# A two-block transformer kernel: six plain projection blocks in place of four around the first attention, 34 Strassen blocks in place of 36

## The chip, the cores and the metric

One program runs on one core of a Trainium2 chip. The metric is device time in microseconds (us) for one launch; lower is better. The engines that matter are TensorE (PE, with its weight loads shown as PEld), VectorE (DVE), ScalarE (ACT), GpSimd (POOL, here mostly an issuer of DMAs) and SyncE (SP, an issuer of DMAs).

## The reference, cut to what matters

```
# d_model 1024, 1024 tokens, w_in has 40 column blocks of 256:
# blocks 0-3 sb_q, 4-7 sb_k, 8-11 sb_v, 12-15 sb_g, 16-31 r_q, r_k, r_v, r_g,
# blocks 32-35 m_sb, 36-39 m_ret
h = rms_norm(x, norm_gain)
proj = h @ w_in                                    # all ten outputs
out_a = merge_heads(stick_breaking_attention(rms_norm(q), rms_norm(k), v)) * silu(sb_g)   # 8 heads of 128
out_b = merge_heads(rms_norm(chunkwise_retention(rotary(q), rotary(k), v))) * silu(r_g)
merged = sigmoid(m_sb + b0) * (out_a @ w_branch_sb) + sigmoid(m_ret + b1) * (out_b @ w_branch_ret)
x = x + merged @ w_out
# then a second layer (gated linear attention + sliding window attention) and a feed-forward of 4096
```

## The kernel before, in words

Each product of h with one column block of w_in (256 columns, "a block") is done in one of two ways. Every operand is split into a high and a low part, and each product is made of three: high by high, high by low, low by high.

- **Strassen blocks** (n = 0 to NPROJ - 1, PE line 2785): seven half-size products of 4 x 3 = 12 matmuls with 512 columns, 84 matmuls in all, in PSUM banks 0 to 3 in turn (`product_bank`, bank (7n + o) % 4). DVE adds the products up, ACT applies what the block's kind asks for (norm, turn, silu, sigmoid, or nothing: "plain" in `proj_kind`), and POOL stores the block to the DRAM tensor `projections`. `content(n)` says where block n goes there, `proj_column` which columns of w_in it takes.
- **Plain blocks** (`gemm`, PE line 621, and `filler`, PE line 2891): four outputs of 24 matmuls, 96 matmuls in all. A matmul of a filler is called a pass.

After the last Strassen block comes the attention of the 8 heads, two heads ("a pair") at a time, 16 steps per pair (`sb_pair`, S = 0 to 15; the even steps are one head, the odd ones the other, with 1 to 8 blocks of 128 keys). In step S, PE makes the scores of step S + 2 (line 2863, and the mask, line 2865), turns the weights of step S (`turn`, 2872) and, after two steps of a head, multiplies by the values (`weigh`, 2844). ACT takes two sigmoids of the scores (`shares`, 1426 and 1429) and copies the turned weights out of banks 0 and 1 (`keep_first`, 1435); DVE makes a running product (`remaining`, 2061) and a product with it (`weights`, 2068). `turn(S)` waits for `weights(S)` and for `keep_first(S - 1)`. The scores of two steps fit in PSUM; bank 2 holds the attended output, bank 3 a background output.

Between these PE runs the passes of plain blocks, in an order written out by hand: `FILL_PASSES[i][S]` passes in step S of pair i, up to three of them ahead of `turn` ("early") and the rest behind `weigh`. When 24 passes are done, ACT copies bank 3 to a staging tile (`keep_filler`, 1442), POOL stores it (line 1117), and only then may the next output begin (`g_raw`). Before, two plain blocks of m_sb are made so, each over two pairs (48 passes for each of the pairs 0 to 2), and the last pair adds one output of the first covering block (72 passes).

After the last pair come the covering blocks (COVER and COVER + 1, two blocks of m_ret): they give PE work while ACT and DVE split the attended output into its parts (`s_hi` 1488, `s_lo` 2094). Then the branch product B1 (line 621 again) needs those parts and its own weights. SP loads weights in the order of use (`load_block`, 593): each load waits until the block two before it is done. The m_sb and m_ret gates are read back later by POOL (`gate_again`). The hidden layer of the feed-forward uses the same Strassen code with block numbers that go on from NPROJ.

Of the kernel before, what the change touches and what calls it, by code (L numbers as in the profile page):

```python
# [5 lines left out]
SEQ, DM = 1024, 1024  # L6
# [53 lines left out]
def build(nc, x, norm_gain, w_in, b_merge, sb_q_gain, sb_k_gain, ret_out_gain, w_branch_sb, w_branch_ret, w_out,  # L60
# [189 lines left out]
    with ctx:  # L250
# [18 lines left out]
        NPROJ = 36  # L269
        NORM0 = 3  # L270
        NHID = 15
        SB_GATE, SB_MERGE = 30, 34
# [4 lines left out]
        ms_d = nc.dram_tensor("merge_gate_sb", (P, KT // 2, SEQ), f32, kind="Internal").ap()  # L277
# [385 lines left out]
        pa_stored = [sem(f"pa_stored{u}") for u in range(2)]  # L663
        mg_in, mg_sig = [sem(f"merge_gate{j}_in") for j in range(4)], sem("merge_gate_sigmoid")
# [10 lines left out]
        L1, COVER, B1, B2, L5 = 0, 2, 4, 8, 12  # L675
        L6, L7, L8 = 16, 26, 30
# [53 lines left out]
        def proj_kind(n):  # L730
            return "plain" if n < NORM0 else "norm" if n < NORM0 + 8 else "turn" if n < NORM0 + 12 or 20 <= n < 24 else "plain" if n < 26 else "silu" if n < 34 else "sigmoid"

        def content(n):
            return 12 + n if n < NORM0 else n - NORM0 if n < NORM0 + 12 else n if n < 24 else n + 10 if n < 26 else n - 2 if n < 30 else n if n < 34 else n - 6

        def proj_column(n):
            m = content(n)
            return BC * (m if m < 12 else m + 4 if m < 28 else m + 8 if m < SB_GATE else m - SB_GATE + 12 if m < SB_MERGE else m - SB_MERGE + 32)
# [54 lines left out]
        HID0, HSUM0 = 32 + 4 * (F0 - 25), 32  # L793
# [9 lines left out]
        def form_stored(b, name):  # L803

            n, two = F0 + b, 16 * (b // 2 + 1)
            if name == "a11":
                return (pa_stored[0], 16 * 8 + two) if b % 2 else (c_stored[0], 16 * 28 + two)
            if name == "a22":
                return c_stored[1], 16 * 28 + 16 * (b + 1)
            if name in ("a12", "s3"):  # L810
                return c_stored[(2 if name == "a12" else 4) + n % 2], 16 * 14 + two
            q = ("s1", "s2", "s4").index(name)
            return q_stored[q], 16 * ((32 - q + 2) // 3) + 16 * (b + 1)
# [39 lines left out]
        def _(sp):  # L853
# [38 lines left out]
            load_block(sp, L1, 0, w1_d[:, :, 8, 2 * BC:3 * BC])  # L892
            sp.wait_ge(product_done, 7 * (NPROJ - 1) + 5)
            attention_values(0)
            load_block(sp, L1 + 1, 1, w1_d[:, :, 8, 3 * BC:4 * BC])
# [171 lines left out]
        def _(pool):  # L1067
# [16 lines left out]
            for n in range(NPROJ):  # L1084
                for j in range(4):
# [14 lines left out]
                    else:  # L1100
                        pool.wait_ge(first_ok, 32 + 4 * (n - 26) + j + 1)
# [6 lines left out]
            for i in range(4):  # L1108
# [16 lines left out]
            for j in range(4):  # L1125
                gate_again(proj_d[SB_MERGE].rearrange("p (c t) -> p c t", c=2), 0, j)
            for b in range(2):
                for j in COVER_ORDER[b]:
# [3 lines left out]
            for b in range(3):  # L1132
                for j in range(4):
                    pool.wait_ge(kept[j], kept_by(B1 + b))
                    if b:
                        gate_again(ms_d, 2 * b - 2, j)
                    else:
                        gate_again(proj_d[SB_MERGE + 1].rearrange("p (c t) -> p c t", c=2), 0, j)
            for u in range(2):
                pool.wait_ge(pa_stored[u], 16 * 8)  # L1140
# [98 lines left out]
        def _(act):  # L1239
# [107 lines left out]
            def gate_bias(n, ct):  # L1347
                c = COLS["merge"] + 8 + 2 * (n - 34) + ct
                return cols[:, c:c + 1] if n >= 34 else 0.0
# [18 lines left out]
            for n in range(1, NPROJ + 1):  # L1368
# [4 lines left out]
                if n == 26:  # L1373
                    act.preload_act_table_set("silu_and_others")
                elif n == 34:
# [42 lines left out]
            def sb_pair(i, n):  # L1418
# [34 lines left out]
                for S in range(16):  # L1453
# [36 lines left out]
            for s in range(2):  # L1490
                for v, j in enumerate(COVER_ORDER[s]):
                    act.wait_ge(gp_done, done(COVER + s, v))
                    act.wait_ge(pa_stored[j % 2], 16 * (4 + 2 * s + v // 2))
# [387 lines left out]
        def _(dve):  # L1881
            for j in range(4):
                dve.sem_inc(kept[j], 1)
            dve.sem_inc(gated, 4)
            dve.wait_ge(own_gain, 16)
# [157 lines left out]
            def end_of_pair(i):  # L2043

                dve.wait_ge(o_kept, 8 * i + 8)
                for j in range(4) if i % 2 else ():
# [1447 lines left out]
```

## Time and profile before

| | |
|---|---|
| median of 3 runs | 2438.62 us (2437.91 to 2439.53) |
| the profiled execution | 2438.28 us, its span 2436.5 us |
| PE busy | 2404.9 us, 12042 matmuls |
| PEld busy | 1973.6 us |
| DVE busy | 1613.6 us |
| ACT busy | 1030.9 us |
| Strassen blocks | about 47 to 743 us of the span |
| attention, 4 pairs | 743 to 962 us |
| covering outputs | 962 to 1000 us |

A busy share of PE is not PE at its peak: a matmul of 512 columns is shown with 0.39 us, though in a steady run one starts every 0.227 us. Rates of PE are therefore read from the time in which a run of matmuls goes by, divided by their number, and stalls from the idle time before a weight load.

### The profile page before, as it was taken

The numbers are of one execution on the slowest core, as the hardware profiler recorded it, in microseconds if no ns is written. First come the engines' busy times: TensorE is split into PE (matmuls) and PEld (weight loads), VectorE is DVE, ScalarE is ACT, GpSimd is POOL, SyncE is SP. The second block draws the span as 40 slices with busy tenths as digits, with TensorE's granted clock in tenths as the row PEclk, the third lists the DMA queues.
The fourth block names the chain that finished last, engine by engine and source line by source line (L and its number), as shares of the span: only waits on it lengthen the run. The fifth ranks groups of instructions, "written<-read, shape, count | busy, mean of one in ns | idle before, by whom it ended". The sixth has DMA issues, their size and how long they took to land.

```text
span 2436.5 us, 30593 instructions
## 1 busy us (share of the span) xinstructions
PE 2404.9 (99%) x12042; PEld 1973.6 (81%) x12042; DVE 1613.6 (66%) x2079; ACT 1030.9 (42%) x1751; POOL 238.9 (10%) x395
## 2 busy tenths in 40 slices
PE   7999999999999999999999999999999999999998
PEld 6888888888887777889888877887888888888887
DVE  7777656556556766377742654267567776789889
ACT  6466422233335656123422346234545444533334
POOL 2011111111110000100010003000001211100000
PEclk9999999999999999999999999999999999999999
DMA  4322333333334231734232410100333444673433
GB/s 154 100 104 100 108 104 108 100 108 108 108 123 145 79 116 63 262 100 178 78 115 89 130 35 20 41 30 18 115 123 123 162 147 158 242 259 141 156 122 120
DMA packets 141775, 285.90 MB, mean 117 GB/s; under 512 B 18470, under 2 KB 91744, under 8 KB 134848
## 3 DMA queue, kind: packets, MB, share of 16 engines
q1 hardware_dynamic: 109168, 175.45, 21.7%
q0 software_dynamic: 32464, 108.49, 12.6%
q8 instruction: 96, 1.57, 0.3%
q14 instruction: 47, 0.39, 0.1%
HBM read 200.02 MB, written 83.89 MB: 117 GB/s over the span
## 4 chain that ended last, share of the span: by engine, by line
PE 90%; DVE 5%; DMA 2%; ACT 1%; DVEq 1%; issue 1%; ACTq 0%; SPq 0%; POOL 0%
PE ps L2785 38%; PE ps L621 13%; PE ps L3466 8%; PE ps L3049 7%; PE ps L2844 2%; PE ps L2863 2%; PE ps L615 2%; PE ps L3356 2%; PE ps L2891 2%; PE ps L2872 1%; PE ps L3341 1%; PE ps L2752 1%; PE ps L2964 1%; PE ps L2979 1%; PE ps L3034 1%
## 5 line engine op out<-in xcount | busy, mean ns | idle before, releaser
L1991 DVE TENSOR_TENSOR proj_out<-ps,proj_out 128x512 f32<-128x512 f32 x334 | 223.3, 685 | 248.9 <-PE ps L2785 234.9
L2785 PE MATMUL ps<-a_hi,pw_hi 128*128 128x512 f32 x600 | 235.2, 392 | 0.0
L2785 PE MATMUL ps<-a_lo,pw_hi 128*128 128x512 f32 x600 | 233.5, 389 | 0.0
L2785 PE MATMUL ps<-t_hi,pw_hi 128*128 128x512 f32 x560 | 219.3, 392 | 0.0
L2785 PE MATMUL ps<-t_lo,pw_hi 128*128 128x512 f32 x560 | 218.0, 389 | 0.0
L2785 PE MATMUL ps<-a_hi,pw_lo 128*128 128x512 f32 x400 | 155.9, 390 | 0.0
L2785 PEld LDWEIGHTS ps<-a_lo,pw_hi 128*128 128x128 f32 x600 | 112.7, 188 | 23.0
L2785 PEld LDWEIGHTS ps<-a_hi,pw_hi 128*128 128x128 f32 x600 | 112.6, 188 | 22.9
L1264 ACT ACTIVATE pw_hi<-pw_raw 128x512 fp32r<-128x512 f32 x150 | 83.6, 621 | 107.4 <-DMA pw_raw<-in_w_in 61.8
L1918 DVE TENSOR_TENSOR pw_lo<-pw_raw,pw_hi 128x512 fp32r<-128x512 f32 x200 | 128.4, 683 | 0.2
L2785 PEld LDWEIGHTS ps<-t_lo,pw_hi 128*128 128x128 f32 x560 | 105.2, 188 | 21.5
L2785 PEld LDWEIGHTS ps<-t_hi,pw_hi 128*128 128x128 f32 x560 | 105.1, 188 | 21.3
L2061 DVE TENSOR_TENSOR_SCAN kept<-kept 128x128 f32<-128x128 f32 (+7 forms) x64 | 86.7, 1355 | 49.6 <-ACT kept L1426 49.6
L3466 PE MATMUL ps<-ws_hi,hidden_hi 128*128 128x512 f32 x288 | 112.3, 390 | 0.2 <-DVE gated_first L2658 0.2
L3466 PE MATMUL ps<-ws_hi,hidden_lo 128*128 128x512 f32 x288 | 112.1, 389 | 0.0
L3466 PE MATMUL ps<-ws_lo,hidden_hi 128*128 128x512 f32 x288 | 112.0, 389 | 0.0
L2785 PE MATMUL ps<-t_hi,ps_lo 128*128 128x512 f32 x280 | 109.1, 389 | 0.0
L2785 PE MATMUL ps<-t_hi,pw_lo 128*128 128x512 f32 x280 | 109.0, 389 | 0.0
L1102 POOL DMA_DIRECT2D projections<-proj_out x112 | 60.6, 541 | 480.9 <-ACT proj_out L1336 167.8
L1271 ACT ACTIVATE pw_hi<-ps_raw 128x512 fp32r<-128x512 f32 x150 | 87.9, 618 | 38.9 <-DVE ps_raw L1910 38.9
L3049 PE MATMUL ps<-w_hi,a_hi 128*128 128x512 f32 x256 | 101.5, 397 | 0.0
L601 DVE TENSOR_TENSOR w_lo<-w_raw,w_hi 128x2048 fp32r<-128x2048 f32 x26 | 59.5, 2288 | 61.5 <-ACT w_hi L597 54.9
(531 smaller groups left out, 6190.4 us busy)
## 6 DMA issues: line engine op xcount, KB each, us to landing
pw_raw<-in_w_in SPq DMA_DIRECT2D x36, 1024.0 KB, 5.8
projections<-proj_out POOLq DMA_DIRECT2D x112, 256.0 KB, 3.5
hidden_raw<-hidden_forms SPq DMA_DIRECT2D x28, 1024.0 KB, 4.8
pw_raw<-in_w_ff SPq DMA_DIRECT2D x16, 1024.0 KB, 6.0
w_quarter<-in_w_ff SPq DMA_DIRECT2D x16, 1024.0 KB, 6.8
hidden_forms<-proj_out POOLq DMA_DIRECT2D x56, 256.0 KB, 3.1
hidden_forms<-nb POOLq DMA_DIRECT2D x56, 256.0 KB, 3.4
w_raw<-in_w_in SPq DMA_DIRECT2D x10, 1024.0 KB, 5.2
```

The costliest lines, as they stand in the source:

```text
L601: dve.tensor_tensor(W_lo[s][:, :, :], W_raw[s][:, :, :], W_hi[s][:, :, :].bitcast(f32), ALU.subtract).then_inc(w_lo, 1)
L615: last = pe.matmul(bank[banks[j]][:, r * BC:(r + 1) * BC], a[:, k, t:t + P], w[s][:, k, :], start=(k == 0 and g == 0), stop=(k == KT - 1 a ...
L621: last = pe.matmul(bank[banks[j]][:, :], w[s][:, k, ct * P:(ct + 1) * P], a[:, k, th * HALF:(th + 1) * HALF], start=(k == 0 and g == 0), s ...
L1102: pool.dma_start(proj_d[content(n)].rearrange("p (c t) -> p c t", c=2)[:, ct, th * HALF:(th + 1) * HALF], PC[out_tile(n, j)][:, :]).then_i ...
L1264: last = act.activation(PWH[s][:, q, :, :], raw_part(s, q), ACT.Copy)
L1271: last = act.activation(PWH[s][:, q, :, :], raw_part(s, q), ACT.Copy)
L1918: last = dve.tensor_tensor(lo_part(s, q), raw_part(s, q), PWH[s][:, q, :, :].bitcast(f32), ALU.subtract)
L1991: return dve.tensor_tensor(out_ap(n, j), product_bank(n, o), src, ALU.add)
L2061: dve.tensor_tensor_scan(k, k, k, 1.0, ALU.mult, ALU.min)
L2785: last = pe.matmul(product_bank(n, o), w, a[:, k0 + k, t], start=(k == 0 and g == 0), stop=(k == 3 and g == 2))
L3049: last = pe.matmul(bank[row_bank(t)], a[:, kk, tok], half_rows(w[s])[:, k, :], start=(s == 0 and k == 0 and g == 0), stop=(s == 1 and k == ...
L3466: last = pe.matmul(bank[4 * ((g + 1) % 2) + t], a[u][:, k, tok], w[u][:, k, :], start=(k == 0 and v == 0), stop=(k == 3 and v == 2))
```

## The change

Two blocks of m_sb that were Strassen blocks become plain ones: NPROJ goes from 36 to 34, and every pair now has a plain block of m_sb of its own in the background (L1 to L1 + 3, 96 passes each). The output of the first covering block that the last pair made goes back to the covering blocks, which are now two whole blocks. The weights of block L1 + i + 1 are loaded during pair i and split in its steps 10 to 13. `keep_filler` now comes in steps 1, 6 and 11 and after step 15. The two staging tiles are handed on by a new semaphore `stage_free` that POOL raises once the stores of a pair have landed. Background passes of the first pair no longer wait for the last output of the last Strassen block. The last `weigh` of the attention and a wait for the last `keep_filler` now stand between the last pair and the covering blocks.

```diff
-        NPROJ = 36
+        NPROJ = 34
-        FILL_PASSES = [(14, 2, 2, 2, 2, 2, 4, 2, 2, 3, 2, 3, 2, 2, 2, 2)] * 3 + [(14, 2, 2, 2, 2, 2, 5, 5, 4, 5, 5, 0, 2, 2, 4, 6)]
-        fill_upto = [[sum(passes[:S + 1]) for S in range(16)] for passes in FILL_PASSES]
-        fill_after = [{S: upto // PASSES - 1 for S, upto in enumerate(fill_upto[i]) if upto % PASSES == 0 and FILL_PASSES[i][S]} for i in range(4)]
-        COVER_ORDER = ((3, 0, 1, 2), (0, 1, 2, 3))
+        FILL_PASSES = (24, 4, 5, 3, 4, 8, 5, 5, 4, 5, 5, 5, 6, 5, 4, 4)
+        fill_upto = [sum(FILL_PASSES[:S + 1]) for S in range(16)]
+        fill_after = {S: upto // PASSES - 1 for S, upto in enumerate(fill_upto) if upto % PASSES == 0}
...
-        L1, COVER, B1, B2, L5 = 0, 2, 4, 8, 12
+        L1, COVER, B1, B2, L5 = 0, 4, 6, 10, 14
...
+                if i < 3:
+                    load_block(sp, L1 + i + 1, (i + 1) % 2, w1_d[:, :, 8, (i + 1) * BC:(i + 2) * BC])
...
-                for ct in range(2):
-                    th = i % 2
-                    pool.wait_ge(g_raw, 2 * i + (1 + ct))
-                    pool.dma_start(ms_d[:, 2 * (i // 2) + ct, th * HALF:(th + 1) * HALF],
-                                   stage[ct][:, :]).then_inc(pa_stored[ct], 16)
+                for j in range(4):
+                    th, ct = j // 2, j % 2
+                    pool.wait_ge(g_raw, 4 * i + (1 + j))
+                    pool.dma_start(ms_d[:, 2 * i + ct, th * HALF:(th + 1) * HALF],
+                                   stage[j % 2][:, :]).then_inc(pa_stored[j % 2], 16)
+                for u in range(2):
+                    pool.wait_ge(pa_stored[u], 32 * i + 32)
+                pool.sem_inc(stage_free, 1)
...
                 def keep_filler(J):
-                    act.wait_ge(gp_done, done(n, 2 * (i % 2) + J))
-                    if i:
-                        act.wait_ge(pa_stored[J], 16 * i)
-                    act.activation(stage[J][:, :], bank[3], ACT.Copy).then_inc(g_raw, 1)
+                    act.wait_ge(gp_done, done(n, J))
+                    if J < 2:
+                        act.wait_ge(stage_free, i + 1)
+                    else:
+                        act.wait_ge(pa_stored[J % 2], 32 * i + 16)
+                    act.activation(stage[J % 2][:, :], bank[3], ACT.Copy).then_inc(g_raw, 1)
...
-                    if S - 1 in fill_after[i]:
-                        keep_filler(fill_after[i][S - 1])
-                    if i % 2 and S in (4, 5):
-                        half_hi(n + 1, (n + 1) % 2, S - 4)
+                    if S - 1 in fill_after:
+                        keep_filler(fill_after[S - 1])
+                    if S in (10, 11):
+                        half_hi(n + 1, (n + 1) % 2, S - 10)
...
-                if i < 3:
-                    keep_filler(1)
+                keep_filler(3)
...
-                    if i % 2 and S in (6, 7):
-                        half_lo(n + 1, (n + 1) % 2, S - 6)
+                    if S in (12, 13):
+                        half_lo(n + 1, (n + 1) % 2, S - 12)
...
-                    pe.wait_ge(*c_kept(NPROJ - 1, 3))
+                    pe.wait_ge(*v_kept(NPROJ - 1))
...
-                    early = first if S - 1 in fill_after[i] or S == 15 and i < 3 else min(first + 3, upto)
+                    early = first if S - 1 in fill_after or S == 15 else min(first + 3, upto)
                     if S == 0 and i == 0:
                         filler(0, upto)
                         scores(2)
+                        pe.wait_ge(*c_kept(NPROJ - 1, 3))
...
-                if i == 3:
-                    filler(fill_upto[3][15], 3 * PASSES - 6)
-                    weigh(3, 7)
-                    filler(3 * PASSES - 6, 3 * PASSES)
 
             for i in range(4):
-                sb_pair(i, L1 + i // 2)
-
-            gemm(pe, COVER, 0, A_hi, A_lo, False, outputs=(0, 1, 2))
+                sb_pair(i, L1 + i)
+            weigh(3, 7)
+            pe.wait_ge(g_raw, 4 * 4)
+
+            gemm(pe, COVER, 0, A_hi, A_lo, False)
             gemm(pe, COVER + 1, 1, A_hi, A_lo, False)
```

The rest of the diff renumbers: `proj_kind`, `content` and `proj_column` for 34 blocks, the semaphore counts that depend on the number of blocks, and the places where the gates are read back.

## Rows read from the trace of the kernel before

**Rows 1.** The page, part 1: busy time of each engine.
```profile
PE 2404.9 (99%) x12042; PEld 1973.6 (81%) x12042; DVE 1613.6 (66%) x2079; ACT 1030.9 (42%) x1751; POOL 238.9 (10%) x395
```

**Rows 2.** The chain in order of time: start us, us, what.
```profile
520.45 209.51 PE ps L2785 x924
...
962.40 38.08 PE ps L621 x168
```

**Rows 3.** Stretches: busy us (x) of PE, PEld, DVE, ACT, POOL; clock, DMA, GB/s.
```profile
520.45:729.96 209.51, 209.51 (x925) 173.44 (x925) 125.69 (x198) 72.79 (x124) 24.57 (x45) 1.00 0.33 110
...
795.00:848.00 53.00, 52.68 (x266) 40.42 (x265) 38.08 (x38) 33.60 (x61) 3.23 (x6) 1.00 0.26 90
...
901.00:962.00 61.00, 60.25 (x303) 47.33 (x302) 37.59 (x37) 34.69 (x62) 3.77 (x7) 1.00 0.25 83
```

**Rows 4.** The chain in pairs 2 and 3: `weigh` of steps 4, 8, 11.
```profile
865.00 0.52 PE ps L2891 x2
865.85 3.25 PE ps L2844 x16
...
879.92 2.38 PE ps L2844 x12
...
888.89 2.38 PE ps L2844 x12
...
919.01 3.25 PE ps L2844 x16
...
934.31 2.38 PE ps L2844 x12
...
943.96 2.38 PE ps L2844 x12
```

**Rows 5.** Waits of the weight loads in the attention: us in total, times, longest.
```profile
PEld ps L2872 <- DVE taken L2068: 4.6, 7, 1.2
PEld ps L2872 <- issue: 4.5, 10, 0.7
```

**Rows 6.** Timeline, PEld at `turn`: start, us, ..., [idle before <- releaser].
```profile
752.30 0.86 PEld L2872 LDWEIGHTS ps<-ident,taken 128*128 128x128 f32 x8 [1.16 <-DVE taken L2068]
...
844.98 0.86 PEld L2872 LDWEIGHTS ps<-ident,taken 128*128 128x128 f32 x8 [0.55 <-DVE taken L2068]
...
847.63 0.14 PEld L2872 LDWEIGHTS ps<-ident,taken 128*128 128x128 f32 x1 [0.24 <-issue]
...
860.35 0.20 PEld L2872 LDWEIGHTS ps<-ident,taken 128*128 128x128 f32 x2 [0.39 <-issue]
...
888.34 0.31 PEld L2872 LDWEIGHTS ps<-ident,taken 128*128 128x128 f32 x3 [0.60 <-issue]
...
898.16 0.86 PEld L2872 LDWEIGHTS ps<-ident,taken 128*128 128x128 f32 x8 [0.92 <-DVE taken L2068]
...
955.13 0.14 PEld L2872 LDWEIGHTS ps<-ident,taken 128*128 128x128 f32 x1 [0.68 <-issue]
```

**Rows 7.** Timeline, ACT: `keep_first` of step 1, pair 1.
```profile
806.32 1.03 ACT L1435 ACTIVATE wt<-ps 128x1024 f32<-128x1024 f32 x1 [1.30 <-PE ps L2872]
```

**Rows 8.** Timeline, ACT in the last pair: `keep_filler`, `keep_first` of step 14, `keep_attended`.
```profile
943.16 0.62 ACT L1442 ACTIVATE stage<-ps 128x512 f32<-128x512 f32 x1
...
953.99 1.02 ACT L1435 ACTIVATE wt<-ps 128x1024 f32<-128x1024 f32 x1 [1.62 <-PE ps L2872]
...
961.05 0.38 ACT L1447 ACTIVATE out_t<-ps 128x256 f32<-128x256 f32 x1 [1.87 <-PE ps L2844]
```

**Rows 9.** Timeline, SP's queue: the loads of the weights of B1 and B1 + 1.
```profile
982.25 18.65 SPq L593 DMA_DIRECT2D w_raw<-in_w_branch_sb  x2
```

**Rows 10.** The chain at the end of the covering blocks: start us, us, what.
```profile
1000.48 0.46 issue
```

**Rows 11.** DMA issues between 742 and 1010 us: KB each, median us to landing.
```profile
w_raw<-in_w_in SPq DMA_DIRECT2D x2, 1024.0 KB, 8.1
```

**Rows 12.** Timeline, ACT: the last output of L8 is kept, bank 3.
```profile
1837.74 0.60 ACT L1800 ACTIVATE proj_out<-ps 128x512 f32<-128x512 f32 x1 [0.74 <-PE ps L621]
```

More of the change, by code:

```diff
@@ L276, in build @@
         x1_d = nc.dram_tensor("x1_saved", (SEQ, DM), f32, kind="Internal").ap()
[L277 removed]
+        ms_d = nc.dram_tensor("merge_gate_sb", (P, KT, SEQ), f32, kind="Internal").ap()
         mr_d = nc.dram_tensor("merge_gate_ret", (P, KT // 2, SEQ), f32, kind="Internal").ap()
@@ L663, in build @@
         pa_stored = [sem(f"pa_stored{u}") for u in range(2)]
+        stage_free = sem("gate_staging_free")
         mg_in, mg_sig = [sem(f"merge_gate{j}_in") for j in range(4)], sem("merge_gate_sigmoid")
@@ L730, in proj_kind @@
         def proj_kind(n):
[L731 removed]
+            return "plain" if n < NORM0 else "norm" if n < NORM0 + 8 else "turn" if n < NORM0 + 12 or 20 <= n < 24 else "plain" if n < 24 else "silu" if n < 32 else "sigmoid"
         def content(n):
[L734 removed]
+            return 12 + n if n < NORM0 else n - NORM0 if n < NORM0 + 12 else n if n < 28 else n + 2 if n < 32 else n - 4
         def proj_column(n):
             m = content(n)
[L738 removed]
+            return BC * (m if m < 12 else m + 4 if m < 28 else m + 8 if m < SB_GATE else m - SB_GATE + 12)
         def x_kept(n):
@@ L806, in form_stored @@
             if name == "a11":
-                return (pa_stored[0], 16 * 8 + two) if b % 2 else (c_stored[0], 16 * 28 + two)
+                return (pa_stored[0], 16 * 12 + two) if b % 2 else (c_stored[0], 16 * 26 + two)
             if name == "a22":
-                return c_stored[1], 16 * 28 + 16 * (b + 1)
+                return c_stored[1], 16 * 26 + 16 * (b + 1)
             if name in ("a12", "s3"):
-                return c_stored[(2 if name == "a12" else 4) + n % 2], 16 * 14 + two
+                return c_stored[(2 if name == "a12" else 4) + n % 2], 16 * 13 + two
             q = ("s1", "s2", "s4").index(name)
@@ L1125, in _ @@
             for j in range(4):
-                gate_again(proj_d[SB_MERGE].rearrange("p (c t) -> p c t", c=2), 0, j)
+                gate_again(ms_d, 0, j)
             for b in range(2):
-                for j in COVER_ORDER[b]:
+                for j in range(4):
                     th, ct = j // 2, j % 2
@@ L1134, in _ @@
                     pool.wait_ge(kept[j], kept_by(B1 + b))
[L1135 to L1138, printed above, removed]
+                    gate_again(ms_d, 2 * b + 2, j)
             for u in range(2):
-                pool.wait_ge(pa_stored[u], 16 * 8)
+                pool.wait_ge(pa_stored[u], 16 * 12)
             pool.wait_ge(ret_scaled, 16)
@@ L1347, in gate_bias @@
             def gate_bias(n, ct):
-                c = COLS["merge"] + 8 + 2 * (n - 34) + ct
-                return cols[:, c:c + 1] if n >= 34 else 0.0
+                c = COLS["merge"] + 8 + 2 * (n - 32) + ct
+                return cols[:, c:c + 1] if n >= 32 else 0.0
             def proj_second(n, j):
@@ L1490, in _ @@
             for s in range(2):
-                for v, j in enumerate(COVER_ORDER[s]):
-                    act.wait_ge(gp_done, done(COVER + s, v))
-                    act.wait_ge(pa_stored[j % 2], 16 * (4 + 2 * s + v // 2))
+                for j in range(4):
+                    act.wait_ge(gp_done, done(COVER + s, j))
+                    act.wait_ge(pa_stored[j % 2], 16 * (8 + 2 * s + j // 2))
                     act.activation(stage[j % 2][:, :], bank[j], ACT.Sigmoid, bias=merge_bias(1, 2 + s, j)).then_inc(kept[j], 1)
@@ L1884, in _ @@
             dve.sem_inc(gated, 4)
+            dve.sem_inc(stage_free, 1)
             dve.wait_ge(own_gain, 16)
@@ L2045, in end_of_pair @@
                 dve.wait_ge(o_kept, 8 * i + 8)
-                for j in range(4) if i % 2 else ():
+                for j in range(4):
                     dve.sem_inc(kept[j], 1)
@@ L2877, in filler @@
                     for m in range(first, upto):
-                        ct, r = divmod(m, PASSES)
-                        th = i % 2
+                        j, r = divmod(m, PASSES)
+                        th, ct = j // 2, j % 2
                         k, g = divmod(r, 3)
-                        if r == 0 and (i or ct):
-                            pe.wait_ge(g_raw, 2 * i + ct)
-                        if r == 0 and th == 0 and ct == 0:
+                        if r == 0 and (i or j):
+                            pe.wait_ge(g_raw, 4 * i + j)
+                        if r == 0 and j == 0:
                             pe.wait_ge(w_lo, n + 1)
-                        s = n % 2
-                        if ct == 2:
-                            s, ct = 0, 1
-                            if r == 0:
-                                pe.wait_ge(w_lo, COVER + 1)
                         w, a = ((W_hi, A_hi), (W_hi, A_lo), (W_lo, A_hi))[g]
-                        last = pe.matmul(bank[3], w[s][:, k, ct * P:(ct + 1) * P], a[:, k, th * HALF:(th + 1) * HALF],
+                        last = pe.matmul(bank[3], w[n % 2][:, k, ct * P:(ct + 1) * P], a[:, k, th * HALF:(th + 1) * HALF],
                                          start=(r == 0), stop=(r == PASSES - 1))
@@ L2898, in sb_pair @@
                     scores(1)
-                    pe.wait_ge(*c_kept(NPROJ - 1, 3))
+                    pe.wait_ge(*v_kept(NPROJ - 1))
                 for S in range(16):
-                    first, upto = fill_upto[i][S - 1] if S else 0, fill_upto[i][S]
-                    early = first if S - 1 in fill_after[i] or S == 15 and i < 3 else min(first + 3, upto)
+                    first, upto = fill_upto[S - 1] if S else 0, fill_upto[S]
+                    early = first if S - 1 in fill_after or S == 15 else min(first + 3, upto)
                     if S == 0 and i == 0:
```

22 lines of the change are left out of this document (11 added, 11 removed).

## The prediction

> **What bounds the kernel now.** I read the page's busy times first. PE is busy 99% of the span and DVE 66% [rows 1], so the question is what PE's time consists of. The chain of waits in order of time answers it for the Strassen blocks: 924 matmuls (11 blocks of 84) in 209.51 us without a break [rows 2], 0.2267 us each. Such a block of a kind that gives PE nothing else costs 84 x 0.2267 = 19.05 us. The covering outputs run at the same rate: 168 matmuls in 38.08 us [rows 2]. The table by stretches says how far the attention is from that. A pair takes about 53 us; in it DVE is busy 38 and ACT 34 us [rows 3], so neither of them is the limit, and the only thing that can be won there is time in which PE stands still. PE's busy time can't show this, because matmul ends are modelled; the idle time ahead of the weight loads can. In the attention the loads of `turn` waited 4.6 us for DVE and 4.5 us for "issue", 17 times in all [rows 5]. A step without a stall shows 0.24 us at this place too [rows 6] (the load at 847.63), so 9.1 - 17 x 0.24 = 5.0 us is all that the whole attention has to give. The granted clock is 1.00 in all three stretches [rows 3], which is the 2.4 GHz level, so there is none to be won by keeping PE busier.
>
> **The change, part by part.** All sums are made against the profiled execution, which took 2438.28 us with a span of 2436.5 us; the median of the runs is 0.34 us above it.
>
> *PE's work.* Two Strassen blocks go: 2 x 84 = 168 matmuls, 38.09 us. They are of the plain kind and leave nothing else behind on PE. Their DVE additions, ACT copies and stores go too, but they lay beside PE's work. Two plain blocks come: 192 matmuls, of which 168 go into the attention (4 x 96 passes in place of 3 x 48 + 72) and 24 into the covering blocks. Twenty-four matmuls more than before are 5.44 us if a pass in the attention costs what it costs elsewhere.
>
> *Does it?* Pairs 2 and 3 differ by their passes alone in two stretches. From the `weigh` of step 4 to that of step 8, pair 3 has 5 passes more (1.13 us) and took 15.30 in place of 14.07 us, +1.23. From there to step 11 it has 3 more (0.68 us) and took 9.65 in place of 8.97 us, +0.68 [rows 4]. So passes are not swallowed by slack; each costs 0.227 us and a little. The little is the change from one form of matmul to another: ten steps of each pair now have a second group of passes, 40 groups. The second stretch puts it at 0 (two groups more, nothing left over); two passes behind the mask take 0.52 us where 0.453 are due [rows 4], 0.07 for a group. I take 0.03, nearer to the measured stretches, +1.2 us (0 to 2.8).
>
> *Stalls that the passes fill.* At the first pair's step 1, PE stood 1.16 us, because DVE waits for the stores of the last block to land [rows 6]; eight more passes (24 for 14 in step 0, none for two in step 1) come ahead of it, so 1.16 - 0.24 = 0.92 us go. At step 14 PE waits for DVE in every pair: 0.55, 0.55, 0.92, and about as much in the last (the 4.6 us of [rows 5] less the 1.16 and the small ones leave 0.65). Eight passes more (1.8 us) come between the scores of step 14 and its `turn`; that is more than any of these, so 2.67 - 4 x 0.24 = 1.7 us go. DVE has to do two more half-block splits in steps 12 and 13, but it stands over 3 us there now. The wait at step 11, 0.60 us for ACT's copy [rows 6], stays: between the scores and this `turn` there are five passes before and after. Together -2.6 us.
>
> *Stalls that it makes.* (a) In pairs 1 to 3 ACT now meets `keep_filler` in step 1, ahead of `shares(3)`. It can't pass it until all 24 passes are done, though the scores were ready 12 passes earlier; then come 0.62 us of copy [rows 8], the two sigmoids and the 1.03 us `keep_first` [rows 7] that `turn(2)` waits for. PE has, from the 24th pass on, `turn(1)`, four passes, the scores of step 4 and three passes, about 3.2 us, against ACT's 3.5. That is 0.3 us a pair, where 0.39 - 0.24 = 0.15 is lost now [rows 6]; pair 0 has its scores later and loses its 0.15. Net +0.3. Queued behind `keep_filler` on ACT are `shares(3)` and `keep_first(1)`; DVE waits for the former, PE for both. (b) In the last pair, one pass in place of three lies between the last long `turn` and `turn(15)`, which waits for a 1.02 us copy [rows 8] and stalled by 0.68 already [rows 6]: +0.45. (c) After the last `weigh` PE now waits for ACT's `keep_attended` and then `keep_filler`, 0.38 + 0.62 us [rows 8], with about 0.3 for the hand-overs; nothing is left to cover it. +1.3 (1.0 to 1.6). Together +2.05.
>
> *Covering blocks and B1.* B1 began 0.46 us late [rows 10], 18.7 us after its weight load was issued at 982.25 [rows 9] and 38.5 us after the cover began. The cover is now 43.5 us long, so the load may be issued up to 24.8 us into it, where it was 19.9: the 0.46 goes. What could eat this is the load of COVER + 1. It was issued early in the last pair; now it waits for the last pass, some 2 us ahead of the cover. With the 8.1 us of [rows 11] it lands at 6 us into the cover, where ACT could begin its split at 2, and everything behind it on ACT (the split of the attended output) moves by 4 us. 19.9 + 4 is still under 24.8. Price: -0.46, and a bound of +1.5 should the landing take 10 us or more.
>
> *At nothing.* The four stores and the wait for their landing on POOL hold up `stage_free`; they are done some 3 us after the pair's last copy, and ACT asks for it after 24 passes, 5.4 us or more. The two more weight loads and splits have a pair each, ahead of a use 20 us or more later. The new bank order puts the first hidden product on bank 2 and the second on bank 3, in place of 0 and 1; bank 3 is kept by 1838.34 [rows 12], and the second product comes 2.7 us behind the first at 1837.7. The background's earlier start in pair 0 gains at most 0.1, since the scores stand ahead of it.
>
> *Sum.* 5.44 + 1.2 - 2.6 + 2.05 - 0.46 = +5.6 us: span 2442.1, the execution 2443.9, on the median 2444.2 us.
>
> **Where a rule speaks otherwise.** PE's loads are busy 173.44 of 209.51 us in the Strassen stretch, 83%, but 40.42 of 53 in a pair, 76% [rows 3]. The Trainium skill (Perfetto Trace Analysis, Identifying the Most-Contended Engine) says to judge TensorE's headroom by this share and not by matmul busy; by that rule a pair has room. Its section Optimization Strategy adds that interleaving regimes with different limits may help, which is what the change does. The row against it is the direct one: in [rows 4] eight more passes took 1.91 us, more than their 1.81. The second rival below prices the rule.
>
> **The rivals.**
> 1. *The stalls go and none come.* All 5.0 us of [rows 5] are filled, the copies of (c) are hidden, and a second group costs nothing: 5.44 - 5.0 - 0.46 = 0.0, 2438.6 us. For it: every pair gets 48 passes to spread. Against it: the schedule puts none of them at step 11 nor ahead of `turn(15)`, and (c) has nothing behind it. Half of it gives 2441.
> 2. *Faster: the loads' idle share is room.* If a pair can be packed to the 83% of the Strassen stretch, 48 more passes of 0.19 us of load make (40.42 + 9.1) / 0.828 = 59.8 us, +6.8 in place of +10.9, and the last pair (47.33 + 4.6) / 0.828 = 62.7, +1.7 in place of 5.4. The attention then grows by 22.1 us and not 38.1: 2438.6 + 5.4 - 16.0 = 2428.0 us. It decides if passes run under the score matmuls, whose loads wait while 512 columns stream. [rows 4] says that they don't.
> 3. *Slower: ACT's order and late weights.* `keep_filler` ahead of `shares(3)` makes a chain of ACT and DVE that PE feels beyond step 2, 1 us in each of three pairs, COVER + 1 lands late enough to cost B1 1.5 us, and groups cost their upper bound: +2.7 + 1.5 + 1.6 on top of 5.6 gives 2450 us at most, 2448 in its middle.
>
> **How the numbers follow.** Forecast 0.62 (2441.5 to 2446.5), rival 1 with its halves 0.15, rival 3 0.20, rival 2 0.03. The range that leaves out 2 in 10 is 2440.5 to 2448.5. A measurement of this kernel tells 0.2% from no change, that is 4.9 us: 2433.7 and 2443.5 are the borders. The forecast lies just above the upper one, so of its 0.62 some 0.37 count as slower; with rival 3 that is 0.57, same 0.40, faster 0.03.
>
> **What would show it.** PE matmuls 12042 + 24 = 12066. The last Strassen block ends 38.1 us earlier; the attention is 36 to 40 us longer, some 256 to 259 us in place of 219; pairs near 63.5 us. The loads of `turn` wait for DVE under 2 us in the attention in place of 4.6. A gap of 1.0 to 1.6 us stands ahead of the first matmul of line 621 in the cover, and no "issue" ahead of B1. I am wrong if a pair grows by clearly less than 10 us (rival 2), if B1 starts late, or if stalls appear at steps 2 to 4 of a pair.

## The result, and the profile after

The changed kernel takes 2443.19 us (median of 22 runs, 2442.18 to 2445.51), the kernel before 2439.14 us in 22 runs beside it (2436.92 to 2441.78). The ratio is 1.0017, 95% interval 1.0011 to 1.0023: 4.05 us slower by the medians. The forecast was 2444.2 us, 5.6 us slower. The profiled execution took 2443.5 us with a span of 2441.7, the one of before 2438.28 with 2436.5.

The page of the changed kernel, busy times (as in [rows 1]):

```profile
PE 2408.4 (99%) x12066; PEld 1977.3 (81%) x12066; DVE 1596.4 (65%) x2047; ACT 1031.0 (42%) x1747; POOL 239.0 (10%) x395
```

Twenty-four matmuls more and 17 us less of DVE's time: the work moved as announced, and DVE's part of it bought nothing.

The changed kernel's chain in order of time (start us, us, what; L2789 are the Strassen products, L2848 is `weigh`, L2867 the scores, L620 the covering blocks):

```profile
684.87 20.63 PE ps L2789 x91
705.78 1.77 PE ps L2867 x4
...
724.75 3.24 PE ps L2848 x16
...
788.34 3.25 PE ps L2848 x16
...
851.93 3.25 PE ps L2848 x16
...
915.51 3.25 PE ps L2848 x16
...
955.82 3.31 PE ps L2848 x16
959.13 0.93 PE ps L2890 x4
960.05 0.67 PE ps L2848 x4
961.02 0.60 ACT stage L1446
```

The `weigh` of step 4 comes round every 63.59 us. In the trace of before it came round every 52.9 us (812.96 to 865.85; the latter is in [rows 4]), so 48 passes more cost 10.7 us, 0.223 us each. The last line is the new wait at the end.

The stretch of one pair in the changed kernel (busy us of PE, PEld, DVE, ACT, POOL; clock; DMA; GB/s), to be held against [rows 3]:

```profile
788.34:851.93 63.59, 63.33 (x313) 49.42 (x313) 38.27 (x39) 35.21 (x63) 4.30 (x8) 1.00 0.29 100
```

The waits of the weight loads from 700 to 1000 us of the changed kernel (L2876 is `turn`), to be held against [rows 5]:

```profile
PEld ps L2876 <- issue: 5.0, 11, 1.3
...
PEld ps L620 <- ACT stage L1446: 1.2, 1, 1.2
```

No `turn` waits for DVE any more. The waits for "issue" include the long one ahead of the last `turn`. Here are some of them (step 11 of pair 0, step 2 of pairs 1 and 2, the last `turn`), and the one ahead of the cover, from the timeline of PEld:

```profile
750.66 0.31 PEld L2876 LDWEIGHTS ps<-ident,taken 128*128 128x128 f32 x3 [0.47 <-issue]
...
781.92 0.20 PEld L2876 LDWEIGHTS ps<-ident,taken 128*128 128x128 f32 x2 [0.39 <-issue]
...
845.51 0.20 PEld L2876 LDWEIGHTS ps<-ident,taken 128*128 128x128 f32 x2 [0.39 <-issue]
...
955.49 0.14 PEld L2876 LDWEIGHTS ps<-ident,taken 128*128 128x128 f32 x1 [1.25 <-issue]
...
961.66 0.19 PEld L620 LDWEIGHTS ps<-a_hi,w_hi 128*128 128x128 f32 x1 [1.15 <-ACT stage L1446]
```

**The ledger**, by landmarks of the two traces. The first scores start at 705.34 in place of 743.38: -38.0 us, two Strassen blocks. From there to the first weight load of the cover 256.3 us in place of 218.6: +37.7. From there to the first update of the retention (1097.07 in place of 1092.82) 135.4 in place of 130.8: +4.6. Together +4.25 us, close to the 4.05 of the medians. The spans differ by another 0.95 us, behind 1420 us, where nothing was changed. The repeats below show that the first of the three figures is only good to a microsecond or more.

### The profile page after: what moved, and what is told of

Read it like the earlier page. It is cut to its first block, busy times and chain, and to the rows that moved or that the text cites. A ratio compares the mean times of both kernels' runs of the same rounds, so it can differ in the third digit from the quotient of the medians.

```text
span 2441.7 us, 30602 instructions
## 1 busy us (share of the span) xinstructions
PE 2408.4 (99%) x12066; PEld 1977.3 (81%) x12066; DVE 1596.4 (65%) x2047; ACT 1031.0 (42%) x1747; POOL 239.0 (10%) x395
## 4 chain that ended last, share of the span: by engine, by line
PE 87%; DVE 6%; DMA 2%; ACT 2%; DVEq 1%; issue 1%; ACTq 0%; SPq 0%; POOL 0%
PE ps L2789 34%; PE ps L620 13%; PE ps L3464 8%; PE ps L3047 7%; PE ps L2890 4%; PE ps L2848 3%; PE ps L2867 2%; PE ps L614 2%; PE ps L3354 2%; PE ps L2876 1%; PE ps L3339 1%; PE ps L2962 1%; PE ps L2977 1%; PE ps L3032 1%; DMA projections<-proj_out 1%
## 5 line engine op out<-in xcount | busy, mean ns | idle before, releaser
L1995 DVE TENSOR_TENSOR proj_out<-ps,proj_out 128x512 f32<-128x512 f32 x320 | 213.4, 685 | 235.1 <-PE ps L2789 221.7
L2789 PE MATMUL ps<-a_hi,pw_hi 128*128 128x512 f32 x576 | 225.7, 392 | 0.0
L2789 PE MATMUL ps<-a_lo,pw_hi 128*128 128x512 f32 x576 | 224.3, 389 | 0.0
L2789 PE MATMUL ps<-t_hi,pw_hi 128*128 128x512 f32 x528 | 207.2, 392 | 0.0
L2789 PE MATMUL ps<-t_lo,pw_hi 128*128 128x512 f32 x528 | 205.5, 389 | 0.0
L2789 PE MATMUL ps<-a_hi,pw_lo 128*128 128x512 f32 x384 | 149.7, 390 | 0.0
L2789 PEld LDWEIGHTS ps<-a_lo,pw_hi 128*128 128x128 f32 x576 | 108.2, 188 | 22.1
L2789 PEld LDWEIGHTS ps<-a_hi,pw_hi 128*128 128x128 f32 x576 | 108.2, 188 | 21.9
L2789 PEld LDWEIGHTS ps<-t_lo,pw_hi 128*128 128x128 f32 x528 | 99.2, 188 | 20.3
L2789 PEld LDWEIGHTS ps<-t_hi,pw_hi 128*128 128x128 f32 x528 | 99.2, 188 | 20.1
L2789 PE MATMUL ps<-t_hi,pw_lo 128*128 128x512 f32 x264 | 102.9, 390 | 0.0
L2789 PE MATMUL ps<-t_hi,ps_lo 128*128 128x512 f32 x264 | 102.9, 390 | 0.0
L596 ACT ACTIVATE w_hi<-w_raw 128x2048 fp32r<-128x2048 f32 x26 | 49.7, 1913 | 118.7 <-DMA w_raw<-in_w_branch_sb 52.5
```

The source lines that it names most:

```text
L1995: return dve.tensor_tensor(out_ap(n, j), product_bank(n, o), src, ALU.add)
L2789: last = pe.matmul(product_bank(n, o), w, a[:, k0 + k, t], start=(k == 0 and g == 0), stop=(k == 3 and g == 2))
```

## The experiments

Most are single profiled executions, read by landmarks inside the trace; the last two were also timed, in 11 runs each. The kernel before took 2438.86 us beside the first four, 2438.58 beside the next four and 2438.63 (21 runs) beside the last three.

**Two repeats.** `r_before` and `r_after` are the two kernels unchanged.

> The kernel before, unchanged, for a second trace of it. If the 0.3 us (attention of the second layer) and 1.0 us (start of the last product) by which the changed kernel is later in its trace behind 1420 us are chance, this trace differs from the first one of before by as much at the same places (a last product that begins 329.4 us after the first hidden product in one trace and 330.5 in another). If they belong to the change, it shows 329.4 us again, within 0.2. Attention again 218.9 us from its first pass region to the cover, within 0.1.

> The changed kernel, unchanged, for a second trace. Attention 256.3 us from the first scores' end to the cover within 0.1, retention 4.25 us later than before; and if the tail's 1.0 us is chance, the last product begins 329.4 to 330.5 us after the first hidden product and not always at 330.5.

`r_before` took 2438.84 us, `r_after` 2443.96. In the first traces the last product (of the feed-forward) began 329.4 us after the first hidden product in before and 330.5 in after; in the repeats it was 330.2 (1837.41 to 2167.64) and 330.1 us (1842.94 to 2173.08). So the last 1 us belongs to the first trace of before, not to the change. Another stretch wanders too: the first scores of the repeats start at 742.7 and 706.1, 0.7 us earlier and 0.8 us later than in the first traces, behind Strassen blocks that are the same in each. Between the repeats the two blocks are worth 36.6 us and not 38.0. Over all traces of kernels with 36 Strassen blocks the first scores start between 742.7 and 745.7 us, with 34 between 704.6 and 706.1. What lies between first scores and retention repeats well: 349.8 us in place of 349.4 for before, 391.5 in place of 391.7 for after. The pairs repeat to 0.1 us (63.54 and 63.55 in `r_after`). So totals of single executions can be off by two or three microseconds, and the stretches below are good to some 0.1 us a pair. The experiments with one execution are judged by their stretches.

**What a pass costs when there are fewer.** `e_half` and `e_few` are the kernel before with passes left out. The edit of `e_half` is shown; `e_few` has 24 in place of 2 and 0 in place of 22.

```diff
                         k, g = divmod(r, 3)
...
+                        if r % 2:
+                            continue
...
-                                         start=(r == 0), stop=(r == PASSES - 1))
-                        if r == PASSES - 1:
+                                         start=(r == 0), stop=(r == 22))
+                        if r == 22:
```

> The kernel before with every second background pass left out (each background output is a sum of 12 products in place of 24, so the sb merge gates and one ret gate are not the reference's). 108 passes fewer in the attention. Theory 1 (PE's own work is the attention's time, a pass costs 0.227 us while something else is not late): a pair goes from 52.9 to 47.5 us plus the stalls that lose their cover, 48 to 50, with the load waits at the turn for DVE and ACT growing from 5 us in all to 10 to 15. Theory 2 (the loads' idle share is room, passes run under the scores): a pair shrinks by only 24 x 0.14 = 3.4 us to 49.5 and the waits at the turn stay at 5 us.

> The kernel before with one background pass left of each 24 (same outputs wrong). 207 passes fewer in the attention. Theory 1: PE's own work in a pair falls to 52.9 - 46 x 0.227 = 42.5 us, and a pair takes 44 to 48 us, since the chain of ACT and DVE through a step, about 3 us, is now bare; the price of a pass is 0.227 between 48 and 96 passes a pair, and falls below 0.15 here. Theory 2: the pass costs about 0.14 everywhere, a pair takes 46.5 us and from 24 to 2 passes the slope is the same as from 48 to 24.

They took 2424.99 and 2424.08 us. The `weigh` of step 4 in `e_half`:

```profile
809.25 3.26 PE ps L2844 x16
...
858.59 3.24 PE ps L2844 x16
```

and in `e_few`:

```profile
809.97 3.26 PE ps L2844 x16
...
858.24 3.25 PE ps L2844 x16
```

Pairs of 49.3 and 48.3 us. And the waits of `turn`, in `e_half`:

```profile
PEld ps L2872 <- issue: 9.5, 16, 1.2
PEld ps L2872 <- DVE taken L2068: 8.2, 7, 2.7
...
PEld ps L621 <- issue: 2.1, 2, 1.8
PEld ps L2844 <- issue: 0.3, 1, 0.3
```

and in `e_few`:

```profile
PEld ps L2872 <- DVE taken L2068: 19.2, 14, 3.4
PEld ps L2872 <- issue: 16.5, 26, 1.7
```

| passes in a pair | 2 | 24 | 48 | 96 |
|---|---|---|---|---|
| a pair, us | 48.3 | 49.3 | 52.9 | 63.6 |
| each further pass up to here, us | | 0.05 | 0.15 | 0.223 |
| load waits at `turn`, whole attention, us | 35.7 | 17.7 | 9.1 | 5.0 |

The slope from 24 to 48 passes, 0.148 us, is by itself what rival 2 gives (0.14). Two things tell theory 1 from theory 2, which is rival 2. Theory 2 had one slope everywhere, and there are three. It also left the waits at 5 us, which is 9.1 less 0.24 for each of 17 places; in `e_half` they are 17.7 less 0.24 for each of 23, 12.2 us, inside the 10 to 15 of theory 1. The 108 passes left out are worth 24.5 us. The attention, from the first scores to the cover (743.68 to 947.85), became 14.5 us shorter. 8.6 us of load idle came back at `turn`, 0.3 us ahead of the last `weigh` and 0.3 us ahead of the cover; 0.8 us were not placed. Another 0.9 us went ahead of B1, whose wait is 1.8 us in place of 0.85. From 48 passes on the slope is nearly PE's full price.

`e_few` came out at a pair of 48.3, just above the 44 to 48 of theory 1. Its total is only 0.9 us below that of `e_half` because its Strassen blocks ended 2.1 us later; its attention is 2.6 us shorter (745.74 to 947.27). The pair is not a bare chain of ACT and DVE. PE is still busy for 42.1 of its 48.3 us, and it waits at ten `turn`s on the mean, not at all sixteen:

```profile
809.97:858.24 48.27, 42.11 (x219) 32.04 (x219) 37.63 (x39) 32.59 (x61) 3.23 (x6) 1.00 0.29 102
```

**The new end of the attention.** `e_tail` keeps the work and puts passes back behind the last `weigh`.

```diff
+        LAST_UPTO = fill_upto[:11] + [fill_upto[10] + v for v in (5, 10, 14, 17, 20)]
...
-                    early = first if S - 1 in fill_after or S == 15 else min(first + 3, upto)
+                    early = first if S - 1 in fill_after or S == 15 and i < 3 else min(first + 3, upto)
...
-            weigh(3, 7)
-            pe.wait_ge(g_raw, 4 * 4)
+                if i == 3:
+                    weigh(3, 7)
+                    filler(4 * PASSES - 4, 4 * PASSES)
...
-            gemm(pe, COVER, 0, A_hi, A_lo, False)
+            gemm(pe, COVER, 0, A_hi, A_lo, False, before=lambda j: pe.wait_ge(g_raw, 4 * 4) if j == 3 else None)
```

> The changed kernel with the end of the attention mended: in the last pair three passes stand ahead of the last turn again, four of the 96 passes are kept behind the last weigh, and the wait for the last background copy stands ahead of the cover's fourth output, the only one that uses its bank, in place of ahead of the first. The same work. If the 1.25 us ahead of the last turn and the 1.15 us ahead of the cover are what the new end costs, the cover begins 1.5 to 2.1 us earlier after the start of the last pair (from its step 4 to the cover 46.2 us before, 44.1 to 44.7 now), and the whole gets that much faster, 2441.5 us. If ACT's late start is then met at the split of the attended output, the gain is given back at B1, which would show a wait.

The cut lines give the last pair its own plan (`LAST_UPTO`), four passes short of 96. 2441.72 us. From the last pair's `weigh` of step 4 (915.19) to the cover's first load (960.36) 45.2 us, in place of 46.15 in the changed kernel: 1.0 us gained, where 1.5 to 2.1 were bid. A wait of 0.7 us now stands ahead of the last `weigh` itself (for ACT's copy out of bank 2), and the last `turn` still waits 0.92 us. No wait showed ahead of B1. That the total came so near the bid of 2441.5 is in part chance: ahead of the retention 1.2 us were gained (1095.84 in place of 1097.07). The end was a real loss, but a small one: the kernel stays about 3 us slower than before.

**ACT's order at the start of a pair (rival 3).**

```diff
-        FILL_PASSES = (24, 4, 5, 3, 4, 8, 5, 5, 4, 5, 5, 5, 6, 5, 4, 4)
+        FILL_PASSES = (20, 4, 6, 5, 5, 8, 5, 5, 4, 5, 5, 5, 6, 5, 4, 4)
```

> The changed kernel with 20 passes in step 0 in place of 24 (steps 0 to 5: 20, 4, 6, 5, 5, 8), so that the first background output is done in step 1 and ACT takes it behind the sigmoids of step 3's scores and not ahead of them. The same work. If ACT's order at the start of a pair costs PE time (rival 3), a pair takes 63.2 us or less in place of 63.6 and the wait of 0.39 us at the turn of step 2 goes. If it costs nothing, the pair stays at 63.6 within 0.1; in pair 0 a wait for the stores of the last block may come back, up to 0.2 us.

2444.89 us. The first output is then done in step 1, its copy one step later; the total stays 96. A pair took 64.0 us (789.26 to 853.28), neither the 63.2 nor the 63.6 that were bid. The wait ahead of the `turn` of step 2 grew from 0.39 to 0.59, and a new one stands ahead of the next pass, which needs bank 3:

```profile
845.19 0.20 PEld L2876 LDWEIGHTS ps<-ident,taken 128*128 128x128 f32 x2 [0.59 <-issue]
...
845.62 0.19 PEld L2890 LDWEIGHTS ps<-a_hi,w_hi 128*128 128x128 f32 x1 [0.22 <-ACT stage L1446]
```

These two, 0.20 and 0.22 us, make up the 0.43 us by which the pair grew. The first pair waits 0.76 us at its step 2, where up to 0.2 was bid.

**A second group in a step.**

```diff
-                    early = first if S - 1 in fill_after or S == 15 else min(first + 3, upto)
+                    early = first if S - 1 in fill_after or S == 15 else upto
```

> The changed kernel with all passes of a step ahead of its turn, no second group behind the weigh, except in the steps that begin a new output and in step 15. The same work, some 40 fewer changes of matmul form in the attention. If a second group costs 0.02 to 0.03 us, a pair loses 0.2 to 0.3 us (63.6 to 63.3); but a turn now comes up to 0.7 us later in its step, ACT's copy after it with it, so waits may appear ahead of the next turn. If changes of form cost nothing, the pair stays at 63.6 or gets longer.

2443.01 us, a pair 63.63 us (787.85 to 851.48). The wait at the `turn` of step 11 grew from 0.47 to 0.71, the one at step 2 went. The bid of 63.3 was missed. Ten groups fewer for each pair, 0.24 us more of wait at step 11 and 0.15 us less at step 2 (0.39 less the 0.24 of a step without a stall) gave the same pair. That puts a group at 0.005 us; by step 11 alone it would be 0.02. More than 0.02 does not fit.

**Whether the waits of before are a lack of passes at their place.** `e_spread` is the kernel before with the same 216 passes.

```diff
-        FILL_PASSES = [(14, 2, 2, 2, 2, 2, 4, 2, 2, 3, 2, 3, 2, 2, 2, 2)] * 3 + [(14, 2, 2, 2, 2, 2, 5, 5, 4, 5, 5, 0, 2, 2, 4, 6)]
+        FILL_PASSES = [(14, 2, 2, 2, 2, 2, 2, 2, 2, 2, 3, 3, 2, 3, 3, 2)] * 3 + [(14, 2, 2, 2, 2, 2, 5, 5, 4, 5, 5, 0, 2, 3, 6, 6)]
```

> The kernel before (36 Strassen blocks, 4 plain ones, 216 passes) with its passes spread otherwise: in pairs 0 to 2 steps 6 and 9 give up three, steps 10, 13 and 14 get one each; in the last pair steps 13 and 14 get three from behind. The same work. If the waits at the turns of steps 11 and 14 and of the last step (0.60, 0.55 to 0.92, 0.68 us of load idle) are a lack of passes at that place, a pair goes from 52.9 to 52.4 us and the whole attention from 218.9 to 216.5, and the kernel is 2 us faster than before. If the passes taken from steps 6 and 9 are missed there, new waits stand at the turns of steps 6 to 10 and the pair stays at 52.9.

2436.56 us. A pair took 52.2 to 52.5 us in place of 52.9 to 53.2, and 216.35 us lay between the first scores (743.85) and the cover (960.20) in place of 218.6, as bid. No wait stands at steps 6 to 10 (pair 2 of `e_spread`, every wait of `turn`):

```profile
859.88 0.20 PEld L2872 LDWEIGHTS ps<-ident,taken 128*128 128x128 f32 x2 [0.39 <-issue]
887.18 0.31 PEld L2872 LDWEIGHTS ps<-ident,taken 128*128 128x128 f32 x3 [0.37 <-issue]
897.00 0.85 PEld L2872 LDWEIGHTS ps<-ident,taken 128*128 128x128 f32 x8 [0.46 <-DVE taken L2068]
899.65 0.14 PEld L2872 LDWEIGHTS ps<-ident,taken 128*128 128x128 f32 x1 [0.24 <-issue]
```

Against [rows 6], step 11 went from 0.60 to 0.37 and step 14 from 0.92 to 0.46, by one pass more ahead of the one and two ahead of the other. Ahead of B1 little was given back. The chain's 0.46 us of [rows 10] is 0.85 us of load idle, the repeat of before has 1.00, and `e_spread` has 0.98:

```profile
1000.91 0.19 PEld L621 LDWEIGHTS ps<-s_hi,w_hi 128*128 128x128 f32 x1 [0.85 <-issue]
...
1000.62 0.19 PEld L621 LDWEIGHTS ps<-s_hi,w_hi 128*128 128x128 f32 x1 [1.00 <-issue]
...
999.25 0.19 PEld L621 LDWEIGHTS ps<-s_hi,w_hi 128*128 128x128 f32 x1 [0.98 <-issue]
```

**The price with the extra matmuls taken out.** `e_short` is the changed kernel without 21 matmuls of the cover.

```diff
-                    for k in range(KT):
+                    ks = 1 if n == COVER and j == 3 else KT
+                    for k in range(ks):
```

> The changed kernel with 21 of the 24 matmuls of the first covering block's last output left out (that ret gate output is wrong), so the plain and Strassen work together is 3 matmuls more than before in place of 24. If the change's price is its 24 matmuls (5.44 us) less what the stalls give back, the cover shrinks by 21 x 0.227 = 4.76 us and the kernel ends 3.7 to 4.8 us earlier, 2438.5 to 2439.5. The lower gain comes about if B1's weights are then what is late: their low part was ready 3.8 us before B1 in the trace of the changed kernel, so 1 us of wait must show ahead of B1, a term that the longer cover hid. If the price lies elsewhere (ACT's order, late weights), more than 1.5 us of wait shows there.

2439.50 us, the span 4.0 us shorter than the changed kernel's. Only 2.7 of these lie ahead of the retention (1094.41 in place of 1097.07); the rest is the wander of the later stretches, so the total met its bid by chance. Of the 4.76 us that were taken out B1's wait gave 2.4 back:

```profile
1002.51 0.19 PEld L621 LDWEIGHTS ps<-s_hi,w_hi 128*128 128x128 f32 x1 [2.38 <-issue]
```

From the cover's first load (961.50) B1's weights took 41.0 us, where before they took 38.9. The wait was bid at 1 us, or at over 1.5 if the late weights of COVER + 1 were in it, and it is 2.4. The trace shows where the 2.1 us arise. ACT splits the weights of COVER + 1 first; in before it could do so 2.4 us after the cover's first load, in `e_short` it waits for them until 3.8:

```profile
964.39 1.92 ACT L597 ACTIVATE w_hi<-w_raw 128x2048 fp32r<-128x2048 f32 x1 [2.95 <-DVE out_t L2052]
...
965.28 1.92 ACT L596 ACTIVATE w_hi<-w_raw 128x2048 fp32r<-128x2048 f32 x1 [3.83 <-DMA w_raw<-in_w_in]
```

The split of the attended output on ACT and DVE follows it and ends 1.4 us later (17.1 in place of 15.7 us after the cover's first load). SP waits for just that (`s_lo`) before it issues the retention's loads and, behind them, the load of B1's weights. This comes at 22.15 us in place of 20.24 ([rows 9]); the retention's loads took 0.5 us longer to issue:

```profile
983.65 17.31 SPq L592 DMA_DIRECT2D w_raw<-in_w_branch_sb  x2
```

The last 0.2 us lie between the issue and B1. In the two traces of the changed kernel the low part of B1's weights is ready 39.8 and 40.4 us after the cover's first load, in the two of before 38.8 and 39.0, in `e_short` 40.9. So the changed kernel has a second cost of some 1 to 2 us that its own longer cover hides.

**Both lessons on the kernel before.** `e_spread_t` is `e_spread` again, `e_best` adds two edits: three passes in the first pair, and the load of B1's first weights ahead of both SP's wait for `s_lo` and the retention's loads. Shown against the kernel before:

```diff
+        FILL_PASSES = [(17, 2, 2, 1, 1, 1, 2, 2, 2, 2, 3, 3, 2, 3, 3, 2)] + [(14, 2, 2, 2, 2, 2, 2, 2, 2, 2, 3, 3, 2, 3, 3, 2)] * 2 + [(14, 2, 2, 2, 2, 2, 5, 5, 4, 5, 5, 0, 2, 3, 6, 6)]
...
             wbr_d = w_branch_ret[0].rearrange("(k p) c -> p k c", p=P)
+            load_block(sp, B1, 0, wbs_d[:, :, 0:BC])
...
-            load_block(sp, B1, 0, wbs_d[:, :, 0:BC])
```

> The kernel before with its passes spread by where PE waits, timed. One look gave 2 us less than before, with 2.3 us less in the attention and 0.5 us given back ahead of B1. If that is the whole of it, ratio 0.9992 (0.9988 to 0.9996).

> The same spread, with three more passes in step 0 of the first pair (one less in steps 3, 4 and 5), where PE waits 1.2 to 1.5 us for the stores of the last block, and with B1's first weight load issued ahead of the retention's loads and not behind them. All work is done. If both waits are what they look like, 0.7 us go at the first pair and the 1.0 us ahead of B1 goes, 1.5 to 1.7 us less than with the spread alone: 2435.0 us, ratio 0.9985. If the retention's loads are then late, a wait of the rotation on DVE moves B1's outputs and the gain ahead of B1 is given back within the B1 blocks.

`e_spread_t`: 2436.52 us, ratio 0.9990 (0.9981 to 0.9999), as bid. `e_best`: 2435.57 us, ratio 0.9987 (0.9978 to 0.9996), 11 runs each. The wait of the first pair in `e_best`, which was 1.16 in before and 1.08 in `e_spread_t`:

```profile
753.44 0.86 PEld L2872 LDWEIGHTS ps<-ident,taken 128*128 128x128 f32 x8 [0.50 <-DVE taken L2068]
```

and the chain through the cover and B1, now without a break:

```profile
960.64 108.82 PE ps L621 x480
```

B1's first weights now land 6 us after their issue (ACT, which waited for them, starts at 983.02), where before ACT had to wait for them until 996.60, 14.4 us after the issue at 982.25 [rows 9]:

```profile
977.01 0.37 SPq L593 DMA_DIRECT2D w_raw<-in_w_branch_sb  x1
...
983.02 1.92 ACT L597 ACTIVATE w_hi<-w_raw 128x2048 fp32r<-128x2048 f32 x1 [2.00 <-DMA w_raw<-in_w_branch_sb]
```

The gain over the spread alone is 0.95 us of the 1.5 to 1.7 bid. The cover began 215.8 us after the first scores (744.48 to 960.25), against 215.9 in `e_spread_t` (743.81 to 959.72): the three passes moved the wait and won 0.1 us net. The wait of step 2 grew from 0.39 to 0.48 us and one of 0.21 us turned up at step 6, the first of the steps behind those that gave up a pass. From the cover to the retention `e_best` is 0.7 us shorter (130.1 in place of 130.8), which is the wait ahead of B1. Both kernels are faster than before by a tenth of a percent, and so than the changed kernel, which is slower than before.

## Why the prediction was right, point by point

The direction, the range and most of the reasons held; the size was 1.5 us too high. By the traces, where the changed kernel loses 4.25 us, the forecast had the attention at +38.7 (measured +37.7) and the cover with B1 at +5.0 (measured +4.6). By its steps:

- **PE's work**: -38.1 us for the Strassen blocks forecast, -38.0 measured in the first traces and -36.6 in the repeats, so the close match is luck. Plain work +43.5 us for 192 matmuls; the pair took 0.223 us for each added pass (0.227 forecast), and the cover's 24 their 5.44. The step on which all rested, that the attention has no slack for passes, was right: `e_half` and `e_few` show where the slack begins, at fewer than 48 passes a pair, and the kernel before stood near its edge.
- **Second groups**: +1.2 us forecast, 40 groups at 0.03. Six such groups stood in the last pair of before already (its steps 7 to 10, 14 and 15), so 34 are new, and `e_onegroup` allows 0.02 each at the most: 0 to 0.7 us. This term was too large.
- **Stalls filled**: -2.6 forecast. The waits of `turn` fell from 9.1 us in 17 places [rows 5] to 5.0 in 11; less 0.24 for each place that is -2.7 us, and this is after the 0.57 us that the last `turn` grew by. So 3.2 us were filled. The step that failed is "the wait at step 11 stays": it fell from 0.60 to 0.47 in pairs 0 to 2 (in pair 3 it was 0.48 and stayed), 0.4 us in all. That the passes of step 14 would drown DVE's wait held in all four pairs, and so did the 0.92 us of the first pair's step 1.
- **Stalls made**: (a) +0.3 forecast at step 2; there was none. It is 0.39 us in pairs 1 to 3, as before, and gone in pair 0, -0.15. The prediction had 0.15 us more in each of pairs 1 to 3, from ACT's copy ahead of the sigmoids. `e_step1` puts the copy behind them and does not win those: PE then waits for the copy itself, ahead of the pass that needs bank 3. It moves four passes as well, so it doesn't isolate ACT's order. (b) +0.45 forecast, 1.25 in place of 0.68 us, +0.57. (c) +1.3 forecast, 1.15 us of load idle.
- **B1**: -0.46 forecast, and no wait is there. The wait of before was 0.85 us as load idle, and 5.44 - 0.85 is the 4.6 us of the ledger, so this term was too small by 0.4. The prediction allowed 4 us of delay for the late weights of COVER + 1. `e_short` shows 1.9 us at the issue of B1's load (22.15 us in place of 20.24), inside that. It costs nothing only because the cover grew by 5.44 us.
- **The rivals**: Rival 1 (all stalls filled, none made) was wrong by the 1.25 and 1.15 us at the end of the attention and by what is left at steps 2 and 11. Rival 2, the one by the loads' idle share: PEld was busy 76% of a pair before [rows 3] and 49.42 of 63.59 us, 78%, in the changed kernel, with PE as full as it gets. The Trainium skill (Perfetto Trace Analysis, Identifying the Most-Contended Engine) names this share, beside the share of peak FLOPs, as what to judge TensorE's headroom by. This case's trace doesn't agree that the idle share was room. It measures the mix: four score matmuls of 512 columns take 1.72 us (the row below, of before), 0.43 us each, and the next load, 0.19 us long, shows "issue" for the other 0.24. Rival 3 had its slow start of a pair wrong. Its late weights were there, but in the changed kernel they cost B1 nothing.

```profile
846.07 1.72 PE ps L2863 x4
```

Not shown: why the Strassen stretch and the feed-forward differ by 0.7 us and more between executions, and how much of the 14.4 us that B1's weights took to land in before is due to the retention's loads issued ahead of them and how much to the loads and stores that ran at the same time.

## What to carry to other kernels

Background work has a price curve, and it can be measured by leaving some of it out: here a mean of 0.05 us a pass from 2 to 24 in a pair, 0.15 from 24 to 48 and 0.223 from 48 to 96, where PE's own rate is 0.227. The same block as Strassen work costs 84 / 96 of a pass's 0.227, 0.198 us for each pass replaced. So the split belongs where the curve crosses 0.198. By these means that is an estimate of around 48 passes a pair; nothing between 24 and 48, or 48 and 96, was measured. Filling the background further only swaps cheap work for dear.

Once PE is full, what is left is not how many passes there are but where they stand: moving three of 48 passes of a pair to the steps whose `turn` waited gave 0.6 to 0.7 us a pair and made the kernel faster by 0.1%, which 168 more passes did not.

A cost can hide behind the change's own extra work. Take the extra work out again (as in `e_short`) before calling the rest free. And look at the order of issue on the engine that loads: the delay arose in a chain from one late load over ACT and DVE to SP, which held B1's load back; issued ahead of that wait, in `e_best`, the same load left B1 no wait at all.

## What the runs showed that was not expected

In this mix PE is full at 76 to 78% of weight-load busy time, because the score matmuls stream for 0.43 us behind a 0.19 us load. A pair with two passes left takes 48.3 us, only 4.6 us less than one with 48: of the 10.4 us that 46 passes take on PE, more than half was free. The later copy of the first background output, which was to spare PE a delay, made a pair 0.4 us longer, since PE then waited for the bank. And a load of 1 MB landed 6 us after its issue in one place of SP's order and 14.4 us in another.
